# One load at a time for the operands of a blocked RWKV-7 scan step

## The reference, cut to what matters

```python
def step(S, inp):
    rt, wt, kt, vt, at, bt = inp
    sa = jnp.einsum('bhvk,bhk->bhv', S, at)
    S = S * wt[:, :, None, :] + sa[..., None] * bt[:, :, None, :] + vt[..., None] * kt[:, :, None, :]
    return S, jnp.einsum('bhvk,bhk->bhv', S, rt)
_, y = lax.scan(step, jnp.zeros((Bn, H, N, N), jnp.float32), xs, reverse=reverse)
```

## Time and profile before

| | us |
|---|---|
| median of 3 runs | 1872.35 |
| lowest and highest of them | 1870.29, 1873.09 |
| the profiled execution | 1872.04 |
| its span, first to last instruction | 1870.2 |

### The profile page before, as it was taken

The page is one execution under the profiler, slowest core; times in us unless marked ns, Lnnn a source line. Parts: engine busy times, 40 slices in busy tenths (PEclk is TensorE's granted clock), DMA queues, the critical chain, the costliest instruction groups (busy, mean ns, idle before and its releaser), DMA issues. The chain is left out here.

```text
span 1870.2 us, 41734 instructions
## 1 busy us (share of the span) xinstructions
PE 1679.8 (90%) x17234; PEld 1274.5 (68%) x17234; DVE 1136.5 (61%) x1971; ACT 844.2 (45%) x1342; POOL 269.6 (14%) x337
## 2 busy tenths in 40 slices
PE   5999999998977889888876997799999999999995
PEld 4677777786754778777765886566666666666762
DVE  4558888846765444564446665655665655665764
ACT  4346666412222334443334211555655555655543
POOL 0020000002120434443332000100000000000003
PEclk8999999999989899999998997899999999999997
DMA  5224454442101211111233117698998998998937
GB/s 166 79 90 132 122 138 132 120 160 111 66 25 43 80 60 60 60 60 60 77 155 134 63 64 290 231 375 356 375 376 341 375 374 357 374 374 342 391 124 283
DMA packets 100356, 355.24 MB, mean 190 GB/s; under 512 B 16775, under 2 KB 56071, under 8 KB 85736
## 3 DMA queue, kind: packets, MB, share of 16 engines
q1 hardware_dynamic: 87528, 306.83, 44.1%
q0 software_dynamic: 8064, 29.36, 4.0%
q10 hardware_dynamic: 4608, 16.78, 2.2%
HBM read 294.75 MB, written 56.10 MB: 188 GB/s over the span
## 5 line engine op out<-in xcount | busy, mean ns | idle before, releaser
L2357 DVE TENSOR_TENSOR e_rl<-proj,e_rh 128x1024 fp32r<-128x1024 f32 x256 | 304.5, 1222 | 144.2 <-ACT e_rh L2293 143.3
L2293 ACT ACTIVATE e_rh<-proj 128x1024 fp32r<-128x1024 f32 x256 | 258.8, 1054 | 48.5 <-PE e_ph L51 29.2
L51 PE MATMUL e_ph<-e_rh,e_xh 128*128 128x512 f32 x512 | 220.4, 430 | 16.7 <-DVE e_rl L2357 14.1
L2274 PE MATMUL e_py<-mix,proj 128*128 128x512 f32 x512 | 225.0, 592 | 0.7 <-issue 0.7
L51 PE MATMUL e_ph<-e_rh,e_xl 128*128 128x512 f32 x512 | 201.1, 393 | 0.0
L51 PE MATMUL e_ph<-e_rl,e_xh 128*128 128x512 f32 x512 | 200.3, 391 | 0.0
L51 PE MATMUL a_b<-a_xh,a_wh 128*128 128x512 f32 x432 | 178.1, 412 | 5.9 <-DVE a_wl L587 3.4
L2274 PEld LDWEIGHTS e_py<-mix,proj 128*128 128x128 f32 x512 | 97.0, 190 | 110.7 <-issue 108.1
L51 PE MATMUL a_b<-a_xh,a_wl 128*128 128x512 f32 x432 | 170.0, 393 | 0.0
L51 PE MATMUL a_b<-a_xl,a_wh 128*128 128x512 f32 x432 | 169.8, 393 | 0.0
L51 PEld LDWEIGHTS e_ph<-e_rh,e_xh 128*128 128x128 f32 x512 | 97.1, 190 | 47.2 <-DVE e_rl L2357 19.8
(11 more groups left out here) (382 smaller groups left out, 3229.4 us busy)
## 6 DMA issues: line engine op xcount, KB each, us to landing
proj<-in_moe_w SPq DMA_DIRECT2D x64, 2048.0 KB, 14.2
mix<-in_moe_w SPq DMA_DIRECT2D x32, 2048.0 KB, 8.5
proj<-scan_operands SPq DMA_DIRECT2D x64, 320.0 KB, 4.2
expert_rows<-e_yo ACTq DMA_DIRECT2D x32, 512.0 KB, 11.1
scan_operands<-late SPq DMA_DIRECT2D x56, 256.0 KB, 2.6
proj<-in_w_in SPq DMA_DIRECT2D x27, 512.0 KB, 4.2
proj<-in_x SPq DMA_DIRECT2D x16, 512.0 KB, 6.6
expert_rows<-proj SPq DMA_DIRECT2D x1, 7680.0 KB, 22.4
```

Of the source, the lines that this page charges most:

```text
L51: m = e.matmul(out, lhs[a], rhs[b], start=first and n == 0, stop=last and n == 2)
L2274: m = e.matmul(py[h][:, :], at[:, k, :], w2[j][:, k, h * HALF:(h + 1) * HALF], start=(k == 0), stop=(k == KF - 1))
L2293: e.activation(rh[s % RING][:, :], piece(j, s), ACT.Copy).then_inc(high, 1)
L2357: e.tensor_tensor(rl[s % RING][:, :], piece(j, s), rh[s % RING][:, :].bitcast(F32), ALU.subtract).then_inc(low, 1)
```

## The change

A wait is put behind each load of a step, from step 2 on. SP issues a load, waits until it has landed (`op_in[j]` counts 64 for every earlier step of the same buffer and 16 for each load), and only then issues the next. The eight loads of steps 0 and 1 are issued as before. The wait stands behind the fourth load too, so SP goes on to its next wait on `op_free`, and after step 15 to `clear_past` and `clear_beyond`, only when all four have landed.

```diff
                         t = i if d == 0 else NT - 1 - i
                         for g in range(GP):
                             e.dma_start(op[j][:, g, d, :, :], S.ops[p + g, d, t, :, :, :]).then_inc(op_in[j], 16)
+                            if n >= 2:
+
+                                e.wait_ge(op_in[j], n // 2 * 64 + (2 * d + g + 1) * 16)
```

## The result

The changed kernel takes 1862.7 us (median; 1855.3 to 1866.5), the kernel before in the same rounds 1872.07. The ratio is 0.9943, 95% interval 0.9927 to 0.9958, so by the ratio the change gains 10.7 us, between 7.9 and 13.7 (the two medians differ by 9.4). The forecast was 5.0. The time lies inside the range of 1862 to 1876, but the gain is more than twice the forecast.

The account below looks back on a forecast made before the run. PE was taken to bound the scan, losing time to late code. From 1872.04 us, code packets took 5.0, the wait and the zeros 0, giving 1867.0; 0.3 for the median made 1867.3, range 1862 to 1876.

Parts of the forecast that it names:

- What bounds the scan: In the scan PE is the bound, busy 20.8 us a step; its main loss is 26.8 us of standstills awaiting code.
- The wait costs nothing: On SP's queue in the scan: four loads one by one take 12.0 us, in time for PE; cost 0.
- The code packets: Behind the scan's loads: smaller bursts delay PE's code less; 12 groups x 0.67 x 5/8 = 5.0 us gained.
- The zeros: The 7,680 KB transfer at the scan's end starts 9.6 us later, its loss moving along; 0, bounds -3.2 to +4.4.
- Nothing to be measured: Rival: in the scan, code waits behind one portion of the operand queue, before as after; 1871 us, chance 0.36.
- Slower, by more code packets hit: Rival: longer loading in the scan hits 3.2 code packets a group; 1877.8 or 1883.5 us; chance 0.13, including zeros falling badly.
- All of it goes: Rival: in the scan the loads' whole excess goes, 8.0 us, giving 1863.3; chance 0.14, including zeros falling well.

Follow-up runs that it names:

- steps 2 to 14 alone: Against the kernel before, waits only behind the loads of steps 2 to 14, step 15's four loads going together: ratio 0.9960.
- half of the change: Against the kernel before, waits only behind step 15's loads (ratio 0.9994), or only behind those of steps 2 to 14 (0.9960).

## Why the prediction was wrong

**What bounds the scan: right.** PE's work stayed, its standstills on "issue" shrank in sum, and their cause is shown by both directions of the dose: 12.5 us of them in A without loads, 22 to 24 with single loads, 25 to 31 with four together, 38.7 with eight. The profile has no row that says that they are waits for code packets; it rests on each of them ending at the same distance behind a packet of its own.

**The wait costs nothing: right.** A load alone took 3.5 us at the median, not 3.0, and no load was waited for.

**The code packets: the step that failed.** The term was 0.67 us a group, times 5/8, times 12 groups: 5.0 us. Measured: 19.6 / 11 = 1.78 us a group, of which 6.9 / 19.6 = 0.35 go, which is 0.63 a group where the term had 0.42. For the same 12 groups that is 7.5 us. The version with steps 2 to 14 alone measured 7.5 as well, but so exact a match is luck: its interval is 4.1 to 10.9, and with single traces the 6.9 us are 2.3 to 10.7. Both factors were off, in opposite directions, and the first by more; this holds with each of the three traces (1.4 to 2.1 us a group, a share of 0.15 to 0.46).
- The size. I took the excess behind the loads over the rest of the same steps. The rest was no undisturbed ground: without loads the rate of these waits is 12.5 / 248.6 = 0.050 us per us, and I had used 0.077. The trace I read had 25.4 us of them where two others had 30.4 and 30.6. And a microsecond of standstill costs more than one of time (19.6 for 16.3), and PE's clock is lower beside long ones. Even my upper bound, 1.5 a group, was below the mean of 1.78.
- The share. Five eighths of the loads' price should have gone, and a third did. The term took each delay to shrink with what stands ahead of the packet. The standstills in A did not become shorter, they became fewer: 31 to 34 where there had been 35 to 43, of 0.71 us in the mean where it had been 0.74. I had asked for none of 1.3 us or more behind the loads, and the changed trace has six in A, as many as the worst of the three traces with four loads. Why fewer and not shorter is open. Single loads disturb the code for 11 to 17 us a step and still hold a code packet back, as the 2.14 us at 743.14 show. I had named this as the slower rival's mechanism; it is at work, at 1.15 us a group, but below what the bursts had cost.

**The zeros: 0 was right in time, within the interval, but not in what they do.** By the times their move with the last group is worth between -2.2 and +4.5 us. I had said that the standstills of 3 to 4 us would move with the zeros. They did not: the longest in B is 2.5 us in both traces of the change, 4.4 and 4.1 before, and B is 6.6 us shorter in the mean. I had left step 15's group out of the count, and no term covered groups that run close to the zeros, though the version without loads has B 9.9 us shorter. Which part of B's gain is the last two groups' and which the zeros' is not told apart. That the zeros cost 7 to 12 us where they run in one block I had put at 8 in the expectations.

**The remainder.** 7.5 us leave 3.2 of 10.7 us. One candidate is the last group with the zeros (1.1). Another is the output stage, whose code is not touched: 152.1 and 152.0 us before, 148.6 and 149.3 after, with PE's clock at 0.87 and 0.89 and its busy time at 133.0 and 130.0 to 130.6 us. The experts' stage gives back 1.3 us of it in the mean. Neither half of the change has the short output stage (151.8 and 152.1 us), which may be why the halves add to less than the whole. What makes the clock differ there was not tested.

**The rivals.** Nothing to be measured: fell. The Trainium skill's rule of turns between queues after each packet ("DMA: Bandwidth & Descriptors", "Queues, rings and completion order") was my reason for it; the dose from four to eight transfers, 20 us by the same number of longer standstills, speaks against a delay that ends with one portion of the queue ahead, though the four added transfers were of another kind. The Trainium skill's rule that code fetch is mostly hidden ("Runtime: NRT & Kernel Launch", "Instruction fetch mechanics") disagrees with all these traces for PE in the scan: even without loads it stands still for 12.5 us in 249. *Slower, by more code packets hit:* fell; the standstills became fewer. *All of it goes:* its 8 us are near the 7.5 that the steps brought, but by another way, since two thirds of the loads' price stayed.

## What to carry to other kernels

Where an engine runs long straight code at a high rate, look for standstills inside runs of equal instructions that wait for nothing; a prefetch that nobody waits for can be their cause, and then its burst is worth breaking up as long as its slack allows. A few pieces that are over soon did at least as well here as the smallest. Spread a large transfer that has no deadline over the steps, but not behind a full burst. And take the price of a disturbance from a run without it: the quiet parts of a disturbed trace are disturbed too. Take more than one trace, and read the clock beside the standstills.

## What was not expected of the hardware

A transfer of 512 KB from the core's memory to DRAM, put behind four loads, cost 1.1 us a step, as much as 1,280 KB from DRAM to DRAM at the same place (both 280.1 us in A against 268.2). The way there differs: 34.5 us of standstills with the clock at 0.96 for the first, 38.7 with 0.98 for the second. Loads of 320 KB that go alone still varied from 2.7 to 5.0 us from issue to landing. And PE's modelled busy time in A, with the same instructions, follows the mean clock: 225.1 us at 1.00 without loads, 229.4 at 0.99 in the kernel before, 231.3 at 0.98 with bursts of eight, 235.6 at 0.96 with pieces behind four loads. The lower level comes beside long standstills: the one of 2.90 us that ends at 860.82 in the kernel before is followed from 862.0 on by 3.4 us at 1.2 GHz, the only ones in its stretch A.
